# The first feed-forward in seven block products per pair of tiles, its modulation sums moved later, and one tap by ScalarE and GpSimd

## The chip, the cores and the metric

One Trainium2 chip, of which the kernel uses one core. The metric is the time of one launch in device microseconds (us). PE is TensorE, DVE VectorE, ACT ScalarE, POOL GpSimd, SP the engine that issues the DMAs.

## What is computed

Two transformer-like blocks run one after the other on 1024 positions of 1024 channels, in float32. The first ends in a feed-forward with a causal convolution of three taps over positions; the second ends in a gated feed-forward without one. D_FF is 2816.

```python
def conv_ffn(h, w_up, dw_w, dw_b, w_down):        # first block, called "f" in the kernel
    u = causal_dwconv(h @ w_up, dw_w) + dw_b      # y_t = sum_k w_k x_{t-2+k}
    gt, v = jnp.split(u, 2, axis=-1)
    return (jax.nn.silu(gt) * v) @ w_down
def swiglu(h, w_gate, w_up, w_down):              # second block, called "g"
    return (jax.nn.silu(h @ w_gate) * (h @ w_up)) @ w_down
mod = silu(c) @ mod_w + mod_b                     # 6 x 1024 columns: shifts, scales, gates
ada = silu(c_2) @ w_ada + b_ada                   # the same for the second block (and for its context)
```

## The kernel before

**Products.** Channels lie on the 128 partitions, positions along a row, so a tile is 128x1024. Each float32 operand is split into an upper part (hi, rounded to the type that TensorE takes, by ACT) and a lower part (lo, the rest, by DVE); a product is hi*hi + lo*hi + hi*lo. A tile of output channels (`tile`, `product`) takes 8 input tiles x 3 terms x 2 halves of 512 positions = 48 matmuls 128x512, the line of which is L904. Weights come by DMA into a ring of RAW = 4 places (`feed`, `raw`), ACT casts them (`wh`, L1549), DVE makes the lower part (`wl`, L2128); three tiles of these are held. PSUM has three accumulators (`ACC`, 1024 columns each) and one more area, `aux`.

**The second feed-forward (g)** has 22 pairs of tiles, gate tile n=0 and value tile n=1. The first two pairs are plain products; three of these four tiles are made "abreast" inside the normalisation that comes before (`block_end`, L950), the fourth, (1,1), by a `tile` of its own. The other 20 pairs (`PAIRS`) are taken as 2x2 block matrices in Winograd's form: seven products ("units" a11, s2, s1, s3, a12, a22, s4) of 4 input tiles x 3 terms = 12 matmuls 128x512 each (L1157), in place of eight. It needs sums of the weights (`weight_sums`, POOL, 4 per pair, 128x512, L3140), of the operand (`operand_sums`, POOL, once, L3149 to L3153) with their upper (`operand_uppers`, ACT, L1649) and lower parts (`operand_lowers`, DVE, L2448), and sums of the results (`combined`, DVE, 7 per pair, L2485). `unit_upper` (L1656) and `unit_lower` (L2453) make hi and lo of a unit's weights, up to six units ahead. Each gated result u is stored to memory by a DMA (`keep`), and read back in the down product (`load_u`, `u_upper`, `u_lower`), which comes in chunks after all pairs (`pairs_down`).

**The first feed-forward (f)** is 44 plain tiles (`ffn`). For each tile ACT multiplies by the newest tap and adds the bias (L1722), and DVE adds the two older taps from PSUM (L2551, L2554); then silu (L1726), product (L2561), hi (L1739) and lo (L2575). u stays on chip in five places, so tiles of the up and of the down product alternate (`ffn_steps`): a down chunk of 4 tiles takes 8 tiles of 24 matmuls. Between the up tiles lie the modulation sums: weight parts of 128x1024 are loaded through the same ring, and DVE adds them up (`modulation_part`, L2152 and L2155: two 128x512 instructions a part, four for the ada parts jb < 4, which carry two rows). Then PE sums over partitions (`modulation_columns`, L1123).

Every engine runs its own list in order. Where an engine waits, everything behind waits.

Of the kernel before, what the change touches and what calls it, by code (L numbers as in the profile page):

```python
# [69 lines left out]
def summed_modulations():  # L70

    parts = [("m", jb, kp) for jb in (10, 11) for kp in range(4)] + [("a", jb, kp) for jb in range(12) for kp in range(4)]
    out, at = {}, (2, 0)
    while parts:
        n = 1 if parts[0][0] == "a" and parts[0][1] < 4 else 2
        out[at], parts = parts[:n], parts[n:]
        at = (at[0], 1) if at[1] == 0 else (at[0] + 1, 0)
    return out
# [5 lines left out]
def summed_at(i):  # L84

    return [(kind, jb) for n in range(2) for kind, jb, kp in SUMMED.get((i, n), ()) if kp == 3]
# [6 lines left out]
def u_at(i):  # L93
# [14 lines left out]
    "pair_dve": ("pu2", "pu3", "pc22", "pu4", "pc11", "pc21", "pc12", "tlo2"),  # L108
    "pair_act": ("hf", "thi2", "p1c"),
    "pair_pool": ("psum", "tsum"),  # L110
# [150 lines left out]

def pool_steps(s):

    return 2 if s < 24 else 0
# [30 lines left out]
def ffn_steps():  # L295

    done = 0
    for c, fs in enumerate(CHUNKS):
        upto = min(fs[-1] + 2, FF)
        while done < upto:  # L300
            yield ("up", done)
            done += 1
        for i in range(ND if c < LAST else 0):
            yield ("dn", c, i)


# [19 lines left out]
PAIR_ORDER = list(pair_slots())  # L326

# [31 lines left out]
class Kernel:  # L359

    def __init__(self, nc, d, mem):
# [5 lines left out]
        self.pt, self.po = Ring(1), Ring(1)  # L367
        self.plan()
# [11 lines left out]
    def half_places(self):  # L380
# [3 lines left out]
        for j, (_, _, split) in enumerate(self.weights):  # L384
# [6 lines left out]
            for unit, size in made:  # L391
# [5 lines left out]
                place += size  # L397

# [44 lines left out]
    def ACC(self, *key):  # L443
        i = self.acc.slot(*key)
        return self.m.ps[:, 1024 * i:1024 * i + 1024]
# [57 lines left out]
    def PSUMS(self, n):  # L503

        return self.F(26, 512, 512 * n)

    def UNIT(self, s, i, u):

        name = UNITS[u]
        if name[0] == "s":  # L510
            return self.PSUMS("s1 s2 s3 s4".split().index(name))
# [23 lines left out]
    def operand(self, u, kk):  # L535

        hi, lo, thi, tlo = TPLACES
# [124 lines left out]
    def norm_plan(self, s):  # L662
        self.aux_take(("spread", s), [("premul", s, ND - 1)], [("premul", s, ND - 1)])
        for i in range(ND):
            self.tmp.take(("pre", s, i), ("prelo", s, i), *([("hf", s, i)] if s == "n4" else []))
# [14 lines left out]
    def ffn_plan(self, s):  # L680
        if s == "g":
            self.pair_plan(s)
            self.last_plan(s)
            return
        for step in ffn_steps():
            if step[0] == "up":
                i = step[1]
                for n in range(2):
# [2974 lines left out]
```

## Time and profile before

| what | value |
|---|---|
| median of 3 runs | 3222.43 us (3219.8 to 3224.1) |
| the profiled execution, its own time | 3218.78 us |
| its span, first to last instruction | 3217.0 us |
| PE, DVE, ACT, POOL busy | 94%, 59%, 34%, 16% |
| f, from tile (1,1) to the end of its down chunks | 623 to about 1290 us |
| g, its 20 block pairs | 2564.5 to 2945.6 us |
| mean granted clock of PE | 0.963 |

A matmul is shown with a duration of about 0.39 us, but the next one starts before it is over; the time that it costs in a full stretch is the distance from start to start. "Idle before" counts how long an engine had nothing to do ahead of a row, and the arrow names who ended that.

### The profile page before, as it was taken

What the parts mean: (1) busy time and instruction counts of PE and PEld (TensorE: products, weight loads), DVE (VectorE), ACT (ScalarE), POOL (GpSimd) and SP (SyncE); (2) the same over time, 40 slices, a digit from 0 to 9 for tenths busy, and PEclk for the clock granted to TensorE, in tenths of its full rate; (3) what the DMA queues carried; (4) which work ended last, traced back from release to release, by engine and by line L of the source; (5) the groups of instructions that cost most, each with busy time, mean ns of one, the idle gap of its engine ahead of it and who ended that gap; (6) DMA issues with size and microseconds to landing.
All of it is one profiled execution on the core that took longest, in us unless ns stands there. A gap on an engine that the chain in (4) does not pass through costs nothing. (4 is left out here: it accounts for less than half of the span.)

```text
span 3217.0 us, 33863 instructions
## 1 busy us (share of the span) xinstructions
PE 3025.4 (94%) x13510; PEld 2448.6 (76%) x13510; DVE 1911.0 (59%) x2135; ACT 1086.4 (34%) x1354; POOL 526.0 (16%) x250
## 2 busy tenths in 40 slices
PE   6999889899999999889999999899999799999997
PEld 4784467678888888768888877677777688887886
DVE  8698884755655554674521077567455866665445
ACT  3456543332222222233221133467323423233221
POOL 0598700000000000000200034000030323220000
PEclk7999889999999999999999999999998899999998
DMA  5215423231222421221332244442232222223232
GB/s 211 60 33 163 164 85 125 82 119 58 92 89 92 130 81 65 99 85 66 133 115 98 101 157 144 113 100 59 84 118 78 85 79 79 85 85 125 72 134 89
DMA packets 103556, 324.33 MB, mean 101 GB/s; under 512 B 11909, under 2 KB 15749, under 8 KB 103207
## 3 DMA queue, kind: packets, MB, share of 16 engines
q1 hardware_dynamic: 103400, 322.17, 30.2%
q8 instruction: 108, 1.77, 0.2%
q14 instruction: 48, 0.39, 0.0%
HBM read 262.87 MB, written 59.24 MB: 100 GB/s over the span
## 5 line engine op out<-in xcount | busy, mean ns | idle before, releaser
L904 PE MATMUL ps<-mainr,wh 128*128 128x512 f32 (+1 forms) x5312 | 1449.5, 390 | 28.6 <-issue 9.2
L904 PEld LDWEIGHTS ps<-mainr,wh 128*128 128x128 f32 x5312 | 995.6, 189 | 237.5 <-issue 32.0
L904 PE MATMUL ps<-mainr,wl 128*128 128x512 f32 (+1 forms) x2656 | 842.6, 389 | 0.0
L904 PEld LDWEIGHTS ps<-mainr,wl 128*128 128x128 f32 x2656 | 502.2, 189 | 103.6
L1549 ACT CAST wh<-raw 128x1024 fp32r<-128x1024 f32 (+2 forms) x272 | 238.7, 882 | 554.9 <-PE ps L904 352.4
L2128 DVE TENSOR_TENSOR wl<-raw,wh 128x1024 fp32r<-128x1024 f32 (+2 forms) x224 | 245.1, 1097 | 296.3 <-ACT wh L1549 296.0
L1157 PE MATMUL ps<-mainr,wh 128*128 128x512 f32 x1120 | 344.9, 389 | 1.5 <-DVE tmp L2468 1.5
L1157 PEld LDWEIGHTS ps<-mainr,wh 128*128 128x128 f32 x1120 | 210.2, 188 | 45.3 <-ACT wh L1656 1.9
L3109 POOL TENSOR_TENSOR tmp<-tmp,mainf 128x1024 f32<-128x1024 f32 x8 | 27.5, 3441 | 1206.1 <-DMA mainf<-in_rope 1142.2
L1157 PE MATMUL ps<-mainr,wl 128*128 128x512 f32 x560 | 217.9, 389 | 0.0
L3076 POOL TENSOR_TENSOR wl<-raw,wh 128x1024 fp32r<-128x1024 f32 x48 | 115.4, 2414 | 416.1 <-ACT wh L1549 416.1
L2620 DVE SCALAR_TENSOR_TENSOR ps<-mainf,vec,ps 128x1024 f32<-128x1024 f32 (+1 forms) x174 | 180.9, 1100 | 2.5 <-ACT ps L1842 2.3
L950 PE MATMUL ps<-mainr,wh 128*128 128x512 f32 x480 | 139.7, 415 | 34.1 <-issue 17.9
L1352 PE MATMUL ps<-mainr,wh 128*128 128x512 f32 x512 | 159.4, 393 | 6.2 <-POOL wl L3076 6.1
L950 PEld LDWEIGHTS ps<-mainr,wh 128*128 128x128 f32 x480 | 95.8, 203 | 60.0 <-issue 35.3
L2485 DVE TENSOR_TENSOR tmp<-tmp,ps 128x512 f32<-128x512 f32 x140 | 94.4, 686 | 76.0 <-PE ps L1157 74.3
L2551 DVE SCALAR_TENSOR_TENSOR tmp<-ps,vec,tmp 128x1023 f32<-128x1023 f32 x44 | 56.3, 1280 | 135.1 <-ACT tmp L1722 135.1
L2966 DVE TENSOR_REDUCE cols<-ps 128x1 f32<-128x1280 f32 x64 | 95.0, 1486 | 45.8 <-PE ps L1417 45.7
L1157 PEld LDWEIGHTS ps<-mainr,wl 128*128 128x128 f32 x560 | 105.1, 188 | 21.9
L1352 PEld LDWEIGHTS ps<-mainr,wh 128*128 128x128 f32 x512 | 96.4, 189 | 27.1 <-issue 6.8
L1722 ACT ACTIVATE tmp<-ps,vec 128x1024 f32<-128x1024 f32 x44 | 52.9, 1205 | 178.0 <-PE ps L904 178.0
L1417 PE MATMUL ps<-mainr 128*128 128x512 f32 (+1 forms) x384 | 96.2, 389 | 16.3 <-DMA mainr<-sc_k 8.4
(301 smaller groups left out, 3622.9 us busy)
## 6 DMA issues: line engine op xcount, KB each, us to landing
raw<-in_ada_w SPq DMA_DIRECT2D x48, 512.0 KB, 3.9
raw<-in_f_up SPq DMA_DIRECT2D x44, 512.0 KB, 4.4
raw<-in_g_up SPq DMA_DIRECT2D x44, 512.0 KB, 3.8
raw<-in_w_in SPq DMA_DIRECT2D x40, 512.0 KB, 4.1
raw<-in_mod_w SPq DMA_DIRECT2D x32, 512.0 KB, 4.1
raw<-in_pw SPq DMA_DIRECT2D x24, 512.0 KB, 3.8
sc_x<-mainf SPq DMA_DIRECT2D x24, 512.0 KB, 2.6
mainf<-sc_x SPq DMA_DIRECT2D x24, 512.0 KB, 7.2
```

Of the source, the lines that this page charges most:

```text
L904: ins = e.matmul(out, wt[:, a:b], xs[n], start=kk == 0 and t == 0, stop=kk == kt - 1 and t == 2)
L950: ins = e.matmul(out, wt[:, a:b], xs[n], start=kk == 0 and t == 0, stop=kk == kt - 1 and t == 2)
L1157: ins = e.matmul(k.PB(s, i, u), wt[:, 128 * kk:128 * kk + 128], xs, start=kk == 0 and n == 0, stop=kk == 3 and n == 2)
L1352: ins = e.matmul(out, wt[:, a:a + 128], x, start=first and t == 0, stop=last and t == 2)
L1417: ins = e.matmul(k.SC[i][:, a:b], k.q_at[u % 3][:, 128 * qt:128 * qt + 128], k.k_at[u % 3][t][:, a:b], start=t == 0, stop=t == 1)
L1549: e.copy(k.WH(j), k.RAWT(j)).then_inc(*k.to("whi", j))
L2128: e.tensor_tensor(k.WL(j), k.RAWT(j), k.WH(j).bitcast(F32), ALU.subtract).then_inc(*k.to("wlo_dve", j))
L2485: e.tensor_tensor(out, x, k.PB(s, i, u), ALU.add).then_inc(*k.to(name, s, i))
L2551: e.scalar_tensor_tensor(out=t[:, 1:T], in0=ps[:, 0:T - 1], scalar=k.V("fdw", 3 * f + 1), in1=t[:, 1:T], op0=ALU.mult, op1=ALU.add).then_i ...
L2620: e.scalar_tensor_tensor(out=out[:, a:b], in0=k.U(i)[:, tap + a:tap + b], scalar=k.V("dww", TAPS * i + tap), in1=k.CVP(i)[:, a:b], op0=ALU ...
L2966: e.tensor_reduce(k.STAT(n, i), k.SC[i], AX.X, ALU.max, negate=True).then_inc(*k.to("atmax", n, i))
L3076: e.tensor_tensor(k.WL(j), k.RAWT(j), k.WH(j).bitcast(F32), ALU.subtract).then_inc(*k.to("wlo_pool", j))
```

## The change

In five parts.

1. f is made as g: pairs 0 and 1 plain, pairs 2 to 21 in seven block products, u stored and read back, all down chunks behind the pairs. `ffn` and `ffn_steps` go.
2. The taps. For a pair, ACT applies the newest tap to both tiles from SBUF (`last_tap`) and multiplies the value tile by its oldest tap (`tap_product`); POOL adds that product (`second_tap`, 128x1022). DVE keeps three of four older taps (`tap`). In pairs 0 and 1 DVE does all four, from PSUM.
3. The operand sums, in f and in g, are made by DVE and not by POOL.
4. The modulation sums: m 10, 11 and ada 0 to 3 in the down steps of f; ada 4 to 11 beside the tiles `w_in` 24 to 37 of the second block.
5. Tile (1,1) of f and of g goes to `aux`, so that it doesn't wait for an accumulator; a dummy Silu after the normalisation loads ACT's table early.

```diff
 def summed_modulations():
-    parts = [("m", jb, kp) for jb in (10, 11) for kp in range(4)] + [("a", jb, kp) for jb in range(12) for kp in range(4)]
+    early = [("m", jb, kp) for jb in (10, 11) for kp in range(4)] + [("a", jb, kp) for jb in range(4) for kp in range(4)]
+    late = [("a", jb, kp) for jb in range(4, 12) for kp in range(4)]
+    steps = [(c, i) for c in range(1, LAST) for i in range(ND)]
+    for n, at in enumerate(steps):
+        out[at] = [early.pop(0)] if n < ND or n % 3 != 1 else []
+    for f in range(24, 38):
+        n = 3 if f in (26, 29, 32, 35) else 2
+        out[f], late = late[:n], late[n:]
...
+        self.beside = {("f_up", 1, 1), ("g_up", 1, 1)}
...
     def block_end(s, hi, shift, copy_free, after):
-            if n == "n4":
-                e.activation(k.F(i), k.TMP("pre", n, i), ACT.Identity, bias=shift(i)).then_inc(*k.to("hf", n, i))
+            tlo = TPLACES[{"n2": "f", "n4": "g"}[n]][3]
+            e.activation(k.F(tlo[i]), k.TMP("pre", n, i), ACT.Identity, bias=shift(i)).then_inc(*k.to("hf", n, i))
+        e.activation(k.COL("dum", 3), m.eps[RMS_EPS], ACT.Silu)
...
 # ScalarE, start of pairs_up
+        if conv:
+            operand_uppers(s, (0, 1))
+            last_tap(0, 0)
+            last_tap(0, 1)
+            operand_uppers(s, (2, 3))
+            conv_gate(0)
+            last_tap(1, 0)
+            uppers(4)
+            conv_gate(1)
+            last_tap(1, 1)
...
 # VectorE, start of pairs_up
-        operand_lowers(s, (0, 1))
-        product(0)
-        operand_lowers(s, (2, 3))
-        lowers(4)
-        product(1)
+        if conv:
+            operand_sums(s, (0, 1))
+            taps(0, 0)
+            operand_sums(s, (2, 3))
+            taps(0, 1)
+            operand_lowers(s, (4, 5, 6, 7))
+            operand_lowers(s, (0, 1, 2, 3))
+            taps(1, 0)
+            lowers(4)
+            product(0)
+            taps(1, 1)
+            product(1)
+        else:
+            operand_sums(s, range(4))
+            product(0)
+            operand_lowers(s, (4, 5, 6, 7))
+            operand_lowers(s, (0, 1, 2, 3))
+            lowers(4)
+            product(1)
...
 # GpSimd
+    def second_tap(i):
+        w.wait_ge(*k.at("cv1", i, 1))
+        w.wait_ge(*k.at("tapm", i))
+        t = k.TMP("cv", i, 1)[:, 2:T]
+        e.tensor_tensor(t, t, k.S(i % 2)[:, 0:T - 2], ALU.add).then_inc(*k.to("tapa", i))
+
+    for i in PAIRS:
+        weight_sums("f", i)
+        if i - 2 in PAIRS:
+            second_tap(i - 2)
...
-    weight_sums("g", PAIRS[0])
-    operand_sums("g", "n4")
-    for i in PAIRS[1:]:
+    for i in PAIRS:
         weight_sums("g", i)
```

The places where the order matters. First DVE's list of the kernel before at the start of f, from the last lower part of the normalisation on: the weights of tile (1,1), then the taps of pair 0 (L2551, L2554), its product and lower part.

```order
L2332 SCALAR_TENSOR_TENSOR mainr_24576_51<-tmp,cols,mainr_16384_50 128x1024
L2128 TENSOR_TENSOR wl<-raw,wh 128x1024
L2551 SCALAR_TENSOR_TENSOR tmp<-ps,vec,tmp 128x1023
L2554 SCALAR_TENSOR_TENSOR tmp<-ps,vec,tmp 128x1022
L2551 SCALAR_TENSOR_TENSOR tmp<-ps,vec,tmp 128x1023
L2554 SCALAR_TENSOR_TENSOR tmp<-ps,vec,tmp 128x1022
L2561 TENSOR_TENSOR tmp<-tmp 128x1024
L2575 TENSOR_TENSOR mainr_8192_61<-tmp,mainr_8192_61 128x1024
L2128 TENSOR_TENSOR wl<-raw,wh 128x1024
```

The same place of the changed kernel, from the operand sums of kk = 2 on (those of kk = 0 and 1 and the taps of tile (0,0) stand ahead of it): L2477 to L2481 are operand sums, L2525 taps, L2487 the lower parts of the operand sums, L2492 those of a unit's weights.

```order
L2477 TENSOR_TENSOR mainf_32768_53<-mainf_32768_53 128x1024
L2479 TENSOR_TENSOR mainf_32768_53<-mainf_32768_53 128x512
L2481 TENSOR_TENSOR mainf_32768_53<-mainf_32768_53 128x512
L2525 SCALAR_TENSOR_TENSOR tmp<-ps,vec,tmp 128x1023
L2525 SCALAR_TENSOR_TENSOR tmp<-ps,vec,tmp 128x1022
L2487 TENSOR_TENSOR mainr_32768_62<-mainf_32768_53,mainr_8192_61 128x1024 x8
L2525 SCALAR_TENSOR_TENSOR tmp<-ps,vec,tmp 128x1023
L2525 SCALAR_TENSOR_TENSOR tmp<-ps,vec,tmp 128x1022
L2492 TENSOR_TENSOR wl<-raw,wh 128x512
```

The weights of the first block product (the last row) now stand behind 12 operand sums, six taps and eight lower parts.

Then DVE's list of the changed kernel at the start of g, where the operand sums (L2477 to L2481; three more such groups are ahead of these rows) came from POOL before:

```order
L2479 TENSOR_TENSOR mainf_8192_58<-mainf_8192_58 128x512
L2481 TENSOR_TENSOR mainf_8192_58<-mainf_8192_58 128x512
L2516 TENSOR_TENSOR tmp<-ps,tmp 128x1024
L2487 TENSOR_TENSOR mainr_8192_61<-mainf_8192_58,mainr_35072_63 128x1024 x2
L2487 TENSOR_TENSOR mainr_8192_61<-mainf_8192_58,mainr_16384_50 128x1024 x2
L2487 TENSOR_TENSOR mainr_8192_61<-mainf_8192_58,mainr_32768_62 128x1024 x4
L2492 TENSOR_TENSOR wl<-raw,wh 128x512
```

Here too all eight lower parts of the operand are ahead of the first weights of a unit; twelve instructions are new on DVE and twelve are gone from POOL.

## Rows read from the trace of the kernel before

**Rows 1.** The page, part 1: busy time, share of the span, instructions.
```profile
PE 3025.4 (94%) x13510; PEld 2448.6 (76%) x13510; DVE 1911.0 (59%) x2135; ACT 1086.4 (34%) x1354; POOL 526.0 (16%) x250
```

**Rows 2.** Windows: length, busy of PE, PEld, DVE, ACT, POOL, clock, DMA.
```profile
623.00:1290.00 667.00, 660.71 (x2976) 548.55 (x2976) 370.42 (x405) 163.64 (x176) 0.00 (x0) 1.00 0.28 91
2564.50:2945.60 381.10, 381.08 (x1680) 315.31 (x1680) 232.89 (x298) 114.44 (x177) 99.46 (x73) 1.00 0.25 82
1700.00:1810.00 110.00, 110.00 (x487) 91.06 (x487) 12.25 (x10) 19.65 (x20) 0.00 (x0) 1.00 0.28 96
```

**Rows 3.** All of PE's waits from 625 to 1285 us: total, times, longest.
```profile
PE ps L904 <- ACT wh L1549: 2.5, 1, 2.5
```

**Rows 4.** PE in order of time, the start of f.
```profile
581.99 2.04 PE L950 MATMUL ps<-mainr,wh 128*128 128x512 f32 x4 [4.71 <-issue]
584.69 1.35 PE L950 MATMUL ps<-mainr,wh 128*128 128x512 f32 x4
...
620.46 0.61 PE L950 MATMUL ps<-mainr,wl 128*128 128x512 f32 x2
623.41 1.15 PE L904 MATMUL ps<-mainr,wh 128*128 128x512 f32 x4 [2.34 <-DVE tmp L2554]
```

**Rows 5.** PE in order of time, the start of g.
```profile
2496.77 2.04 PE L950 MATMUL ps<-mainr,wh 128*128 128x512 f32 x4 [4.71 <-issue]
...
2545.33 0.61 PE L950 MATMUL ps<-mainr,wl 128*128 128x512 f32 x2
2549.40 2.04 PE L904 MATMUL ps<-mainr,wh 128*128 128x512 f32 x4 [3.45 <-ACT tmp L1670]
...
2554.66 1.12 PE L904 MATMUL ps<-mainr,wh 128*128 128x512 f32 x4
...
2564.51 0.70 PE L1157 MATMUL ps<-mainr,wh 128*128 128x512 f32 x2 [1.48 <-DVE tmp L2468]
```

**Rows 6.** DVE and ACT in order of time, start of f and of g.
```profile
619.53 1.23 DVE L2128 TENSOR_TENSOR wl<-raw,wh 128x1024 fp32r<-128x1024 f32 x1 [2.94 <-ACT wh L1549]
...
2524.55 3.39 DVE L2318 TENSOR_TENSOR mainf<-mainf,mainf 128x1024 f32<-128x1024 f32 x1
...
2543.04 3.88 ACT L1649 CAST mainr<-mainf 128x1024 fp32r<-128x1024 f32 x4
2551.26 4.61 DVE L2448 TENSOR_TENSOR mainr<-mainf,mainr 128x1024 fp32r<-128x1024 f32 x4
```

**Rows 7.** POOL in order of time, operand sums at the start of g.
```profile
2516.37 2.39 POOL L3149 TENSOR_TENSOR mainf<-mainf 128x1024 f32<-128x1024 f32 x1 [31.54 <-ACT mainf L1641]
...
2523.46 3.39 POOL L3149 TENSOR_TENSOR mainf<-mainf 128x1024 f32<-128x1024 f32 x1 [1.12 <-ACT mainf L1641]
```

**Rows 8.** DVE's groups by shape, 2565 to 2945 us: busy, mean ns, idle before.
```profile
L2453 DVE TENSOR_TENSOR wl<-mainf,wh 128x512 fp32r<-128x512 f32 x77 | 63.0, 819 | 70.3 <-ACT wh L1656 69.9
L2453 DVE TENSOR_TENSOR wl<-raw,wh 128x512 fp32r<-128x512 f32 x58 | 55.0, 948 | 0.4
```

**Rows 9.** DVE's groups by shape, 640 to 1290 us.
```profile
L2155 DVE SCALAR_TENSOR_TENSOR st<-raw,cols,st 128x512 f32<-128x512 f32 x123 | 91.2, 750 | 4.8 <-DMA raw<-in_mod_w 0.5
L2551 DVE SCALAR_TENSOR_TENSOR tmp<-ps,vec,tmp 128x1023 f32<-128x1023 f32 x40 | 51.2, 1280 | 135.1 <-ACT tmp L1722 135.1
L2585 DVE TENSOR_TENSOR mainf<-mainf,ps 128x1024 f32<-128x1024 f32 x32 | 39.0, 1220 | 75.2 <-PE ps L904 75.2
L2128 DVE TENSOR_TENSOR wl<-raw,wh 128x512 fp32r<-128x512 f32 x32 | 21.9, 685 | 1.9 <-ACT wh L1549 1.9
```

**Rows 10.** ACT's group of the newest tap, 600 to 1290 us.
```profile
L1722 ACT ACTIVATE tmp<-ps,vec 128x1024 f32<-128x1024 f32 x44 | 52.9, 1205 | 178.0 <-PE ps L904 178.0
```

**Rows 11.** PE's waits at the change to g's down product, 2940 to 3110 us.
```profile
PE ps L904 <- DVE wl L2128: 1.4, 1, 1.4
PE ps L904 <- DVE mainr L2459: 1.1, 1, 1.1
```

**Rows 12.** DMA issues: KB each, median us to landing.
```profile
raw<-in_ada_w SPq DMA_DIRECT2D x48, 512.0 KB, 3.9
```

More of the change, by code:

```diff
@@ L840, in plan @@
             tmp.take(("gs", f), (f"gate{f % 2}", f))
+            self.sums_plan(f)
+            for what in summed_at(f - 1):
+                self.aux[0].take(("dmc", *what), ("mod", *what, 0))
         for o in range(2):
@@ new lines, in conv_gate, with uppers @@
+        def conv_gate(i):
+            t = k.TMP("cv", i, 0)
+            w.wait_ge(*k.at("cv", i, 0))
+            e.activation(t, t, ACT.Silu).then_inc(*k.to("us", s, i))
+        def uppers(n):
+            nonlocal made
+            for unit in PAIR_ORDER[made:n]:
+                unit_upper(s, *unit)
+            made = max(made, min(n, len(PAIR_ORDER)))
+        if conv:
+            operand_uppers(s, (0, 1))
[7 more added lines that the diff above has]
+            last_tap(1, 1)
+        else:
+            gate(0)
+            operand_uppers(s, range(4))
+            gate(1)
+            uppers(4)
@@ L1692, in pairs_up @@
+            uppers(n + 6)
+            if after:
+                if conv and u < 2:
+                    last_tap(after, 1 - u)
+                    if u == 0:
+                        tap_product(after)
+                elif conv and u == 4:
+                    conv_gate(after)
+                elif not conv and u == 1:
+                    pair_gate(after)
             if i == PAIRS[-1]:
@@ L2511, in pairs_up @@
             if u == 6:
+                if i == PAIRS[-1]:
+                    for f in CHUNKS[0]:
+                        u_lower(s, f, slots)
                 combined("pc21", i, c21, c21, 5, "pu3")
             lowers(n + 6)
+            if after and conv:
+                if u == 0:
+                    tap(after, 1, 1)
+                elif u < 3:
+                    tap(after, 0, u)
+                elif u == 5:
+                    product(after)
             if i == PAIRS[-1]:
@@ L2886, in vector_program @@
     for f in range(24, 40):
-        split_to(k.W["w_in", f] + 3)
+        split_to(k.ahead("w_in", f))
+        for what in summed_at(f - 1):
+            modulation_sum_add(*what)
     v2 = lambda ap: ap.rearrange("p (n c) -> p n c", c=512)
@@ L3390, in sync_program @@
     for f in range(24, 40):
-        feed(k.W["w_in", f] + RAW)
+        feed(max(k.W["w_in", f] + RAW, k.ahead("w_in", f)))
         if f == 24:
```

498 lines of the change are left out of this document (223 added, 275 removed).

## The prediction

> **What bounds the kernel now.** I read the page first: PE is busy 94% of the span, nobody else over 59% [rows 1]. Then the windows by stage. In f, from 623 to 1290 us, PE is busy 660.7 of 667 us at a granted clock of 1.00, DVE 370 us and ACT 164 us [rows 2]; and of PE's waits between 625 and 1285 us there is one, 2.5 us long [rows 3]. So in this stage the end is set by the number of matmuls and by nothing else. The second feed-forward shows what the new form does where it stands already: its 20 pairs take 381.1 us with 1680 matmuls and PE busy all of it [rows 2]. That is 19.06 us a pair and 0.2268 us from one matmul's start to the next. DVE is busy 232.9 us there, 11.6 us a pair, and POOL 99.5 us, 5.0 us a pair [rows 2]. Last I looked at the joints, where PE does wait: at the start of f tile (1,1) starts 2.3 us late [rows 4], and at the start of g PE idles several times up to 2564.51 us [rows 5].
>
> **The change part by part.** The sum is made against the profiled execution, 3218.8 us by its own time; the median of the runs is 3.6 us higher.
>
> *Fewer matmuls.* Twenty pairs at 84 in place of 96: 240 fewer, at 0.2268 us, **-54.4 us**. PE has no wait to hide them behind, so all of it is on the path as long as the other engines keep up.
>
> *Do they keep up inside a pair?* DVE does what it does in g (11.6 us a pair [rows 2]) and three taps at 1.28 us [rows 9], together 15.5 us. POOL's new add of 128x1022 is near its add of 128x1024, 2.39 us [rows 7], and there is a price for running it beside DVE. The row shows it: at 2524.55 DVE's add of two SBUF tiles took 3.39 us instead of 1.2, and it ended 1.1 us after POOL's instruction, which ran from 2523.46 to 2526.85 [rows 6, 7]. In g's pairs it shows in the unit lower parts: 135 of them took 118.0 us, at 0.685 us alone [rows 9] they would take 92.5, so 25.5 us, a quarter of POOL's 99.5, is DVE waiting [rows 2, 8]. At the same share the new add costs DVE 0.6 us a pair, at most its whole 2.4: 16.1 to 17.9 us, under 19.06. I take 16.5. PE runs up to five units ahead of need (13.6 us), so a late tap by itself stops nothing. ACT gets three instructions of about 1.2 us [rows 10] on top of 5.7 us a pair [rows 2]: 9.3 us. The cost to PE is nothing; the cover is 2.5 us of DVE a pair, 1.2 at the bound.
>
> The Trainium skill, SBUF — State Buffer, section "Who interferes with whom", says that a DVE instruction with two SBUF inputs contends with a GpSimd instruction that reads SBUF, each shutting the other out for its whole length. This speaks against the change, since the taps of a pair now read SBUF where they read PSUM; by the rule with every microsecond of POOL waited for, the sum would be that of the fourth rival below. The trace agrees that the lock exists.
>
> *The start of f.* Here the new order costs. Times are in the trace of before. The three tiles abreast end at 621.1 [rows 4]; tile (1,1) now starts at once, not at 623.4 (**-2.3 us**), and ends 48 matmuls later, at 632.0. The first unit needs its lower part, and DVE comes to it only after its list in the order shown. Its weights for (1,1) are done at 620.8 [rows 6]. Operand sums: one 128x1024 and two 128x512 per kk on DVE; no row has them there, the nearest are its adds, 1.2 us [rows 9] and 0.69 us, so 2.6 us. Two of them end at 626.0. The taps of (0,0) wait for ACT, which first casts the second pair of sums (2 x 0.97 [rows 6]) and then makes the newest tap (1.2 [rows 10]): 629.1. Two taps 631.7, two more sums 636.9, two taps 639.5, eight lower parts at 1.15 (four took 4.61 [rows 6]) 648.7, two taps 651.3, the first unit's lower part 652.0. PE stands still from 632.0 to 652.0, **+20.0 us**; bounds 16 (no wait for ACT) and 26 (each dependent instruction 0.2 us more). After that PE starts at the low clock. After 4.7 us idle six matmuls took 2.70 us instead of 1.36 [rows 4], after 3.4 us idle twelve took 5.3 instead of 2.7 [rows 5]: 1.3 to 2.5 us, I take **+2.0**.
>
> *From the pairs to the down product of f.* g has two waits there, 1.4 and 1.1 us [rows 11]. In f DVE and ACT have besides the last pair's taps in their lists ahead of the weights of the fourth down tile: ACT about 7.7 us after the last unit to its silu, DVE 9.0 to the product, then the copy of a result and the cast, the lower part at 10.7. PE has three down tiles of 12 matmuls ready, 8.2 us. **+2.5 us**, bounds 0 and 9.
>
> *The modulation sums.* The same instructions, moved; the columns on PE are as many. In f's down steps one ada part is four instructions of 0.75 us [rows 9], 3.0 us. A step with everything (weights 0.69, add 1.22 [rows 9], lower part of u 1.22, part 3.0) is 6.1 us against PE's 24 matmuls, 5.44; but over eight steps DVE needs 5.5 + 9.8 + 4.9 + 16 = 36.2 of 43.5 us, and weights are made two tiles ahead, so nothing waits. The ring of four places now holds two down steps: a load (3.9 us [rows 12]), the part and the weights must fit in two steps, 7.6 of 10.9 us. At `w_in` DVE is busy 12 of 110 us [rows 2]; two or three parts a tile of 10.9 us add 3 to 4.5 us. Zero for both.
>
> *The start of g.* POOL's operand sums collided with DVE's normalisation. Without them the chain runs as in f, where the tiles abreast took from 582.0 to 621.1; so in g from 2496.8 [rows 5] to 2535.9, not 2545.9. Tile (1,1) no longer waits for ACT's silu (3.45 us [rows 5]) and ends at 2546.8. Then PE waits for DVE: weights of (1,1) 2535.6, four operand sums 2546.0, product 2547.2, eight lower parts 2556.4, unit 2557.1. With 2.0 us for the clock PE has done the same work by 2559.1 instead of 2564.5: **-5.4 us**, bounds -8 and 0.
>
> *The sum.* -54.4 - 2.3 + 20.0 + 2.0 + 2.5 - 5.4 = **-37.6 us**, or 3181.2 for a profiled execution and 3184.8 for the median. I say 3185.
>
> **The rivals.**
> 1. *The joints cost more.* DVE's one list in front of f's first unit and behind its last one takes the bounds above, 26, 2.5 and 9 us, and g gains nothing: -54.4 - 2.3 + 26 + 2.5 + 9 = -19 us, 3203. For it: at these places every engine waits for another one. Chance 0.13.
> 2. *The down steps of f stall.* The cover of the sums is used up if a load takes longer than 7.2 us with three streams (weights, parts, u) at once; at 1 us a step with a part, 24 of them cost 24 us: -14 us, 3209. Against it: 3.9 us at the median [rows 12]. Chance 0.09.
> 3. *The joints are cheap.* If the sums and taps ahead of the first unit take less than the rows say, or what PE loses there is given back by waits that go elsewhere, f's start costs 8 us less and the end nothing: -48 us, 3174 (down to -60, 3162, with no gap at all). Chance 0.10.
> 4. *DVE and POOL together become the bound (slower than before).* One mechanism: the lock. POOL would work 5.0 + 2.4 = 7.4 us a pair; if DVE waited for all of it and not for a quarter, a pair took 15.5 - 1.3 + 7.4 = 21.6 us, 2.6 more than PE's, 51 us over 20 pairs: -37.6 + 51 = +13 us, 3236. It begins to count at 19.06 us a pair and ends the gain at 20.9. Against it: g's share of a quarter, and the 7 sums of results that read PSUM. Chance 0.04.
>
> The forecast has 0.64. Its own range is 3176 to 3196: the gap of f between 16 and 26, the joint between 0 and 9, g between -8 and 0, not all at one end. To hold 8 in 10 the range reaches over part of rivals 1 and 3: 3168 to 3206. 0.2% or 6.4 us is about what can be told from no change in this kernel; faster 0.92 (the forecast, 1, 3, nearly all of 2), same 0.03, slower 0.05 (rival 4 and what I don't see).
>
> **What would show it.** 1872 instead of 2112 matmuls in f's up product and pairs 19.1 us apart with PE busy throughout; DVE below 18 us a pair. One idle stretch of PE near 20 us before the first unit, ended by DVE's lower part, after a tile (1,1) without a wait. In g, no DVE add above 1.3 us in the normalisation and a gap near 10 us before the first unit. No waits of PE over 1 us in the down steps and at `w_in` 24 to 37. The prediction is wrong if pairs are further apart than 19.1 us, if PE waits for `wl` in the down steps, or if the gap is far from 20 us.

## The result

The changed kernel took 3179.95 us (median of 4 runs, 3174.6 to 3184.8), the kernel before, on the same chip, 3221.38 us (4 runs, 3219.8 to 3224.1): a ratio of 0.987 with a 95% interval of 0.9852 to 0.9889, 41 us less. The forecast was 3185 in a range of 3168 to 3206. The profiled execution took 3174.6 us, its span is 3172.8 us, 44.2 less than before.

### The profile page after: what moved, and what is told of

It reads as the page before. It is cut to its first block and busy times, and to the rows that moved or that the text cites. A ratio compares the mean times of both kernels' runs of the same rounds, so it can differ in the third digit from the quotient of the medians.

```text
span 3172.8 us, 34294 instructions
## 1 busy us (share of the span) xinstructions
PE 2968.9 (94%) x13270; PEld 2403.7 (76%) x13270; DVE 2109.6 (66%) x2387; ACT 1177.8 (37%) x1512; POOL 687.1 (22%) x338
## 5 line engine op out<-in xcount | busy, mean ns | idle before, releaser
L914 PE MATMUL ps<-mainr,wh 128*128 128x512 f32 (+1 forms) x4032 | 1104.8, 390 | 18.0 <-DVE wl L2148 8.3
L914 PEld LDWEIGHTS ps<-mainr,wh 128*128 128x128 f32 x4032 | 753.9, 189 | 175.4 <-issue 21.2
L1154 PE MATMUL ps<-mainr,wh 128*128 128x512 f32 x2240 | 693.9, 391 | 29.7 <-DVE wl L2492 19.7
L914 PE MATMUL ps<-mainr,wl 128*128 128x512 f32 (+1 forms) x2016 | 645.1, 388 | 0.0
L1154 PEld LDWEIGHTS ps<-mainr,wh 128*128 128x128 f32 x2240 | 422.7, 189 | 118.5 <-issue 30.5
L1154 PE MATMUL ps<-mainr,wl 128*128 128x512 f32 x1120 | 437.4, 391 | 0.0
L3159 POOL TENSOR_TENSOR mainf<-raw 128x512 f32<-128x512 f32 x80 | 121.7, 1521 | 659.6 <-DVE wl L2492 302.1
L1154 PEld LDWEIGHTS ps<-mainr,wl 128*128 128x128 f32 x1120 | 211.5, 189 | 44.2
L2541 DVE TENSOR_TENSOR tmp<-tmp,ps 128x512 f32<-128x512 f32 x280 | 187.7, 683 | 81.4 <-PE ps L1154 78.9
L2492 DVE TENSOR_TENSOR wl<-mainf,wh 128x512 fp32r<-128x512 f32 x160 | 135.8, 851 | 84.6 <-ACT wh L1657 84.1
L1657 ACT CAST wh<-mainf 128x512 fp32r<-128x512 f32 x160 | 99.2, 622 | 221.7 <-PE ps L1154 221.7
L2619 DVE TENSOR_TENSOR mainf<-mainf,ps 128x1024 f32<-128x1024 f32 x64 | 78.1, 1220 | 131.3 <-PE ps L914 131.2
L1355 PE MATMUL ps<-mainr,wh 128*128 128x512 f32 x512 | 159.4, 393 | 6.3 <-POOL wl L3117 6.1
L960 PE MATMUL ps<-mainr,wh 128*128 128x512 f32 x480 | 138.0, 411 | 28.8 <-issue 18.2
L1657 ACT CAST wh<-raw 128x512 fp32r<-128x512 f32 x120 | 74.6, 623 | 183.9 <-PE ps L1154 183.9
L960 PEld LDWEIGHTS ps<-mainr,wh 128*128 128x128 f32 x480 | 94.2, 199 | 54.1 <-issue 29.8
```

Source lines behind the costliest of these rows:

```text
L914: ins = e.matmul(out, wt[:, a:b], xs[n], start=kk == 0 and t == 0, stop=kk == kt - 1 and t == 2)
L960: ins = e.matmul(out, wt[:, a:b], xs[n], start=kk == 0 and t == 0, stop=kk == kt - 1 and t == 2)
L1154: ins = e.matmul(k.PB(s, i, u), wt[:, 128 * kk:128 * kk + 128], xs, start=kk == 0 and n == 0, stop=kk == 3 and n == 2)
L1355: ins = e.matmul(out, wt[:, a:a + 128], x, start=first and t == 0, stop=last and t == 2)
L1657: e.copy(k.WH(unit), k.UNIT(s, i, u)).then_inc(*k.to("whi", unit))
L2492: e.tensor_tensor(k.WL(unit), k.UNIT(s, i, u), k.WH(unit).bitcast(F32), ALU.subtract).then_inc(*k.to("wlo_dve", unit))
```

## The profile after

The page, part 1, of the changed kernel (before: [rows 1]):

```profile
PE 2968.9 (94%) x13270; PEld 2403.7 (76%) x13270; DVE 2109.6 (66%) x2387; ACT 1177.8 (37%) x1512; POOL 687.1 (22%) x338
```

PE has 240 matmuls less, all others have more to do. The windows (length, busy time of PE, PEld, DVE, ACT, POOL, clock, DMA) of f's pairs, g's pairs and the stretch with `w_in`, against [rows 2]:

```profile
654.50:1036.00 381.50, 381.49 (x1670) 315.58 (x1671) 349.60 (x360) 177.52 (x238) 176.23 (x95) 0.99 0.24 84
2519.40:2902.80 383.40, 383.34 (x1680) 316.98 (x1680) 235.59 (x301) 114.47 (x177) 104.48 (x76) 0.99 0.25 83
1634.00:1810.00 176.00, 176.00 (x814) 146.67 (x813) 64.87 (x87) 35.80 (x36) 4.79 (x2) 1.00 0.53 191
```

PE is busy all the time in each. In f DVE is busy 349.60 us in 20 pairs, 17.5 a pair, and POOL 8.8 a pair (forecast 16.5 and 7.4). PE in order of time at the two starts (f, then g; before [rows 4] and [rows 5]) and its waits over the whole span:

```profile
654.51 1.19 PE L1154 MATMUL ps<-mainr,wh 128*128 128x512 f32 x2 [19.65 <-DVE wl L2492]
2519.43 1.19 PE L1154 MATMUL ps<-mainr,wh 128*128 128x512 f32 x2 [10.04 <-issue]
```
```profile
PE ps L914 <- DVE wl L2148: 8.3, 6, 2.0
PE ps L960 <- DVE mainr L2357: 6.1, 10, 0.6
```

The first unit of f comes after 19.65 us in which PE stands still, that of g after 10.04. PE's waits for DVE in the normalisation ahead of g (L2357) are 0.6 us each; in the kernel before two of them were longer, this one and one of 2.81 us:

```profile
2524.77 2.05 PE L950 MATMUL ps<-mainr,wh 128*128 128x512 f32 x4 [3.78 <-DVE mainr L2332]
```

DVE in order of time ahead of f's first unit, in the changed kernel:

```profile
622.37 1.23 DVE L2148 TENSOR_TENSOR wl<-raw,wh 128x1024 fp32r<-128x1024 f32 x1 [2.95 <-ACT wh L1548]
...
631.94 2.60 DVE L2525 SCALAR_TENSOR_TENSOR tmp<-ps,vec,tmp 128x1023 f32<-128x1023 f32 x2 [3.17 <-ACT tmp L1687]
...
642.14 9.16 DVE L2487 TENSOR_TENSOR mainr<-mainf,mainr 128x1024 fp32r<-128x1024 f32 x8
651.22 2.60 DVE L2525 SCALAR_TENSOR_TENSOR tmp<-ps,vec,tmp 128x1023 f32<-128x1023 f32 x2
653.73 0.68 DVE L2492 TENSOR_TENSOR wl<-raw,wh 128x512 fp32r<-128x512 f32 x1
```

This is the list as it was costed: the weights of tile (1,1), the wait for ACT's newest tap, eight lower parts, two taps, the unit's lower part; from the end of the first row's instruction (623.6) to the last row's 30.8 us pass, and 31.2 were forecast (620.8 to 652.0).

**Where the time went.** Between events that both kernels have, the 44.2 us of the span are:

```
from the start to the columns in f's normalisation (565.24 -> 567.70)      +2.5
from there to the first waited matmul of L1204   (823.3 -> 776.0)         -47.3   forecast -32.2
from there to the columns in g's normalisation  (1091.4 -> 1098.7)         +7.3   forecast  0
from there to the end                            (737.1 -> 730.4)          -6.7   forecast -5.4
```

The +2.5 lies ahead of everything that the change touches; in the profiled executions of the changed kernel and its variants these columns begin at 565.5 to 570.7 us. The sum was off by 6.6 us, but the stage by stage reading was off by 15 and 7 us with opposite signs. Each row comes from one execution of each kernel. In the repetition of the changed kernel (after_again) the last three stretches are 779.9, 1096.5 and 730.6 us. So f's stretch is uncertain by some 4 us, and the one behind it took between 1096.1 and 1102.0 us over all executions of the changed kernel and of the variants that leave it alone. Within this the old and new profiles show the reasons.

First, the eight late groups of columns. In each the kernel has four float32 matmuls of 128x1, which sum a part of the modulation over the partitions; the trace shows each of them as two instructions, so eight a group and 64 in all. They stood in f and stand at `w_in` now:

```profile
1667.72 0.94 PE L1134 MATMUL ps<-ones,mainf 128*128 128x1 f32 x8
1668.53 1.19 PE L914 MATMUL ps<-mainr,wh 128*128 128x512 f32 x4
```

A group holds PE for 0.81 us (0.85 by the experiment below). Eight of them are -6.8 us in f and +6.8 us later: no gain or loss in sum, but two errors in the stage sums. (That 6.8 is so near the measured 7.3 is in part chance, by the spread above.) The forecast moved only the DVE part of this work.

Second, f's old end. The last up tile ended at 1286.7, ACT's and DVE's taps of it followed, and PE's first matmul of the last chunk came 4.09 us later, at 1290.76. PE in the kernel before, at the wait of [rows 3] and at this one:

```profile
664.28 2.05 PE L904 MATMUL ps<-mainr,wh 128*128 128x512 f32 x4 [2.54 <-ACT wh L1549]
...
1290.76 0.70 PE L904 MATMUL ps<-mainr,wh 128*128 128x512 f32 x2 [4.09 <-issue]
```

The window in which I read PE's waits ended at 1285 us [rows 3]. The two views of the prediction already disagreed: up to 1290 us PE is idle for 667.0 - 660.7 = 6.3 us [rows 2], and the one wait is 2.5. With the new order the pairs are all done before the chunks, so this wait is gone, and so are the 2.5 us of [rows 3] and 0.3 us: -6.9. The low clock behind the two waits went with them (granted clock 0.61 from 664.2 to 668 us, 0.72 from 1290 to 1296): matmuls started 0.43 us apart in place of 0.23, which cost 1.4 us behind the first wait and 1.3 behind the second.

## The experiments

In the tables "first unit" and "end" are counted from the start of the columns of 128x2 in g's normalisation (L1028, L1038 in the changed kernel) in the profiled execution.

**The changed kernel once more** (after_again).

> The changed kernel once more, to have its runs beside the variants and to see how far its runs lie apart (before they lay between 3219.8 and 3224.1, after between 3174.6 and 3184.8). My theory: the spread is in the granted clock of stretches after PE's idle times, of which this kernel has one more of 20 us; so I expect 3180 again, runs 8 to 10 us apart, and a gap of 19 to 20 us ahead of f's first unit in every trace. The rival, that the first four runs were odd: runs within 4 us.

3179.69 us (3175.1 to 3180.2), ratio 0.987 (0.9857 to 0.9884). The runs lie 5.1 us apart, between the theory's 8 to 10 and the rival's 4. The gap is 19.67 us again, so it belongs to the kernel. The first unit comes at 657.8 in place of 654.5, and the difference lies ahead of the gap: what I expected of the clock behind the gap was wrong. The span is 4.7 us longer, and 4 us of it show on PE behind f's down product. PE in order of time, first the changed kernel, then the repetition:

```profile
1294.30 1.16 PE L1081 MATMUL ps<-ident,cols 128*128 128x128 f32 x8 [0.78 <-DVE mainf L2400]
...
1312.37 1.75 PE L1051 MATMUL ps<-cols,tmp 128*128 128x2 f32 x8 [2.94 <-ACT tmp L1786]
```
```profile
1298.73 2.08 PE L1081 MATMUL ps<-ident,cols 128*128 128x128 f32 x8 [0.78 <-DVE mainf L2400]
...
1319.09 1.05 PE L1051 MATMUL ps<-cols,tmp 128*128 128x2 f32 x8 [2.93 <-ACT tmp L1786]
```

The same eight matmuls, behind the same wait of 0.78 us, take 1.16 us in one execution and 2.08 in the other, the lower level of the clock; with the work after them 18.07 us pass to the next long wait in the one and 20.36 in the other. The wait is not what lowers the clock. In both executions it falls ahead of the wait, while PE is busy and has not waited for some 240 us: the granted clock is 1.00 from 1286 to 1288 us, 0.50 from 1290 to 1292 and 0.99 from 1292 to 1294 in the changed kernel, and in the repetition 1.00 from 1288 to 1290 and 0.50 from 1290 to 1302. In the kernel before it stays at 1.00 through this work (1329 to 1341 us). The changed kernel loses 1.5 us by it ahead of the wait.

**The oldest tap back on DVE** (taps_vector).

```diff
 # GpSimd
     for i in PAIRS:
         weight_sums("f", i)
-        if i - 2 in PAIRS:
-            second_tap(i - 2)
-    for i in PAIRS[-2:]:
-        second_tap(i)
 # ScalarE
-                    if u == 0:
-                        tap_product(after)
 # VectorE
+                elif u == 3:
+                    tap(after, 1, 2)
```

> The changed kernel with the oldest tap of the value tile made by VectorE again; ScalarE's product and GpSimd's add are gone, nothing else is changed. Theory A (the matmuls bound a pair, and VectorE has just room): VectorE loses 2.4 to 2.9 us a pair of waiting for GpSimd's add and gains a tap of 1.28 us, so it is busy 16 to 17.5 us a pair, PE waits for nothing and the time is that of the changed kernel within 2 us. Theory B (the move of the tap is what makes seven products possible, VectorE being full without it): VectorE goes past 19.06 us a pair, PE waits for lower parts in the pairs, at 0.5 us a pair or more 10 us slower.

3177.26 us (3174.9 to 3178.9), ratio 0.9865 (0.9852 to 0.9879): not different from the changed kernel. The window of f's pairs in this kernel, below it DVE's group of the unit's lower parts from loaded weights (busy, mean ns), and then the same group and POOL's new one in the changed kernel:

```profile
655.60:1037.10 381.50, 381.46 (x1672) 315.74 (x1673) 350.35 (x380) 160.28 (x219) 121.23 (x76) 0.99 0.24 84
```
```profile
L2489 DVE TENSOR_TENSOR wl<-raw,wh 128x512 fp32r<-128x512 f32 x59 | 49.9, 847 | 0.0
```
```profile
L2492 DVE TENSOR_TENSOR wl<-raw,wh 128x512 fp32r<-128x512 f32 x59 | 71.6, 1214 | 0.0
...
L3165 POOL TENSOR_TENSOR tmp<-tmp,st 128x1022 f32<-128x1022 f32 x19 | 55.6, 2927 | 13.4 <-DVE tmp L2525 13.4
```

DVE is busy 350.35 us with the tap and 349.60 without it. The 19 taps that it gave away were 24.2 us (1.27 each); beside the 55.0 us that POOL works more (176.2 against 121.2) DVE waits 23.4 us more, 22 of them in these lower parts. The part of the change that its title names last, one tap by ScalarE and GpSimd, moved nothing that can be told from the spread of the runs.

**POOL's add twice** (pool_twice).

```diff
         e.tensor_tensor(t, t, k.S(i % 2)[:, 0:T - 2], ALU.add).then_inc(*k.to("tapa", i))
+        if i < FF - 2:
+            w.wait_ge(*k.at("tapa", i))
+            x = k.S(i % 2)[:, 0:T - 2]
+            e.tensor_tensor(x, x, x, ALU.add).then_inc(*k.to("tapd", i))
```

> The changed kernel with a second add of 128x1022 on GpSimd behind the tap's add in pairs 2 to 19 (it spoils the content of a scratch tile, so the next product of the tap starts from it only after it is done; the result is not changed, since the product overwrites it). GpSimd works 2.4 us a pair more. Theory A (VectorE waits for about a third of what GpSimd works): VectorE 17.5 us a pair becomes 18.3, under 19.06, no wait of PE, the changed kernel's time within 2 us. Theory B (the lock is paid in full, and VectorE is 1.5 us from being the bound): VectorE 19.9 us a pair, 18 pairs at 0.8 us, 15 us slower, with PE waiting for lower parts of units.

3183.66 us (3180.0 to 3183.7), ratio 0.9883 (0.987 to 0.9897), some 4 us more than the changed kernel in the same comparison. The window of f's pairs, and DVE's second tap:

```profile
655.40:1036.90 381.50, 378.00 (x1650) 310.52 (x1651) 370.38 (x350) 169.00 (x234) 216.20 (x113) 0.99 0.23 81
```
```profile
L2525 DVE SCALAR_TENSOR_TENSOR tmp<-tmp,vec 128x1022 f32<-128x1022 f32 x18 | 52.3, 2905 | 0.0
```

POOL works 40 us more, DVE is busy 20.8 us more: its second tap, which took 1271 ns, takes 2905. DVE is now at 370 of 381.5 us, and PE begins to wait, 3.5 us in eight waits, one a pair from 889 us on. What ends each of them is ACT's cast of a unit's weights (L1657), which stands in ACT's list behind a silu (L1704) that waits up to 8.0 us for DVE's tap: DVE's delay reaches PE through ACT. So DVE pays 43% (23.4 of 55.0 us) in the one experiment and 52% in the other of what POOL works beside it, between the quarter that the forecast took from g and the whole of the fourth rival; and 17.5 us a pair leave 1.5 us of cover. The Trainium skill, SBUF — State Buffer, section "Who interferes with whom", calls the pair of ports that the two engines share an exclusive lock, and a DVE instruction with two SBUF inputs contends for it with a GpSimd instruction that reads SBUF. The lower parts (0.85 to 1.21 us) and taps (1.27 to 2.91 us) that grow beside POOL's add agree with that; how large a share of POOL's time this costs, the page does not give; the runs do.

**The first units earlier** (units_first). The weights of the first unit are made before all operand sums are cast and lowered, and the taps of (0,1) and (1,0) behind it. In g likewise, with the first product behind the lower parts. ACT's list is reordered to match; the excerpt shows DVE's list in f alone.

```diff
 # VectorE, f
-            operand_sums(s, (0, 1))
+            operand_sums(s, (0,))
             taps(0, 0)
-            operand_sums(s, (2, 3))
-            taps(0, 1)
+            operand_sums(s, (1, 2))
+            lowers(1)
+            operand_sums(s, (3,))
             operand_lowers(s, (4, 5, 6, 7))
+            lowers(2)
+            taps(0, 1)
             operand_lowers(s, (0, 1, 2, 3))
-            taps(1, 0)
             lowers(4)
+            taps(1, 0)
```

> The changed kernel with another order of the same instructions at the start of f and g: the weights of the first two units are split between the operand sums and their lower parts, ScalarE makes the newest taps of pair 0 first, the taps of tile (1,0) come behind the lower parts. Theory A (what PE waits for is only the length of VectorE's list ahead of the first unit): in f the first unit starts right behind tile (1,1), the second at about 642 and the third at about 650 us in the time of the first trace, so PE is 9 to 10 us ahead; in g the first unit fits in the gap, and the second starts at about 2551, 4 to 5 us ahead. In all 13 to 15 us faster than the changed kernel, less 2 for the clock: 3167. Theory B (the gap has another cause, the stores or ScalarE): the gap stays near 20 us and the time near 3180.

3163.73 us (5 runs, 3160.5 to 3168.4), ratio 0.9825 (0.9812 to 0.9839), 16 us less than the changed kernel. PE in f, later in the same kernel:

```profile
643.35 0.91 PE L1154 MATMUL ps<-mainr,wh 128*128 128x512 f32 x2 [4.70 <-DVE wl L2494]
651.00 1.19 PE L1154 MATMUL ps<-mainr,wh 128*128 128x512 f32 x2 [3.07 <-issue]
```

The gap of 19.65 us has become waits of 4.70 and 3.07 us, that of g two of 2.3 and 2.5. So the gap was made by the order of the lists (DVE's, with ACT's along with it), not by the amount of work.

**Both: first units early, taps on DVE** (best: the two edits together).

> The order of units_first (3163.7 us, 16 faster than the changed kernel) together with the oldest tap on VectorE as in taps_vector (2.4 us faster than the changed kernel, which is within the spread of the runs). If the two are independent and the second is real: 3161. If the second is noise: 3164. If ScalarE and GpSimd were needed for the tap when PE has less idle time to catch up in (VectorE enters the pairs with its list less far ahead): PE waits in the first pairs, 3166 or more.

3159.3 us (3159.0 to 3161.4), ratio 0.9815 (0.98 to 0.983): the fastest version by its median, 60 us or 1.9% under the kernel before in the same set of runs (3219.31 us), and without the tap on ScalarE and GpSimd. The intervals of this ratio and of units_first (0.9812 to 0.9839) overlap, so that giving the tap back gains anything is not shown.

**The late columns once** (late_columns_once). This kernel leaves out three quarters of eight sums of the modulation over the partitions, so its output is not the reference's: one matmul of 128x4 stands for four of 128x1 in each of the eight late groups (two instructions in the trace for eight).

```diff
+        if kind == "a" and jb >= 4:
+            src = k.MSUM(kind, jb, 0)[:, 0:128]
+            e.matmul(ps[:, 3072:3076], src, m.ones[:, 0:4], start=True, stop=True).then_inc(*k.to("dmc", kind, jb))
+            return
```

> The changed kernel with one matmul in place of four in each of the eight sums over partitions that moved to the tiles w_in 24 to 37 (it leaves out three quarters of those sums, so the shifts, scales and gates that come from ada 4 to 11 are not the reference's). In the trace f became 47 us shorter and the part behind it, up to the normalisation of g, 7.3 us longer. Theory A (the 7.3 us are the eight groups of columns themselves, 0.9 us each, which f no longer has): 8 x 0.6 = 5 us faster than the changed kernel, and that part 2 us longer than before the change. Theory B (the loads and VectorE's parts beside w_in slow something down): no change.

3171.33 us (3169.5 to 3172.0), ratio 0.985, span 3169.3. PE at the first group and at the last, and below it the last one of the changed kernel:

```profile
1667.89 0.28 PE L1134 MATMUL ps<-ones,mainf 128*128 128x4 f32 x2
...
1800.17 0.28 PE L1134 MATMUL ps<-ones,mainf 128*128 128x4 f32 x2
```
```profile
1804.96 0.94 PE L1134 MATMUL ps<-ones,mainf 128*128 128x1 f32 x8
```

Between the first and the last group 132.28 us pass in place of 137.24: 0.71 us for each of seven groups. The one with four columns itself takes 0.14 us (1800.17 to the next start, 1800.31), so a group of four single columns costs 0.85. The medians differ by 8 us, the spans by 3.5, and eight groups give 5.7; I don't read more into the medians, as the medians of the kernel before differ by 3.4 us from set to set of runs (3218.3 to 3221.7).

**Tile (1,1) without a place of its own** (no_beside).

```diff
-        self.beside = {("f_up", 1, 1), ("g_up", 1, 1)}
+        self.beside = set()
```

> The changed kernel with tile (1,1) of f and of g in the accumulator of tile (0,0) again, the other units' halves moved along. My sum priced this at 2.3 us in f. Looked at again, the first unit waits for VectorE's list at 652 whenever tile (1,1) ends before that, so in f a later tile (1,1), which must now wait for both taps of (0,0), 634.5, only eats into the gap: first unit at the same time, 0 us. The rival, the price as I had it: 2 us slower; or more, if the units' halves are now free later.

3178.67 us (3175.3 to 3180.4), ratio 0.9872. PE at f's start:

```profile
635.57 2.04 PE L914 MATMUL ps<-mainr,wh 128*128 128x512 f32 x4 [10.77 <-DVE tmp L2522]
655.40 1.19 PE L1151 MATMUL ps<-mainr,wh 128*128 128x512 f32 x2 [7.04 <-issue]
```

One gap of 19.65 us has become two of 10.77 and 7.04, and the first unit starts 87.2 us behind the columns of f's normalisation in place of 86.8. The 2.3 us that the forecast booked for the missing wait of tile (1,1) buy nothing by themselves: whatever PE does early ahead of this gap, the gap grows by.

**g's operand sums back on POOL** (g_sums_pool).

```diff
 # VectorE, g
-            operand_sums(s, range(4))
             product(0)
 # GpSimd
+    weight_sums("g", PAIRS[0])
+    operand_sums("g", range(4))
```

> The changed kernel with g's operand sums made by GpSimd again, behind its weight sums of pair 2, as in the kernel before; f keeps them on VectorE. My theory (the 5.4 us of g came from this move alone): adds of the normalisation in g take up to 3.4 us again, tiles abreast end 10 us later; tile (1,1) now waits for nothing, VectorE's list ahead of the first unit is 10.4 us shorter; so the first unit starts about 5 us later than in the changed kernel, counted from the first tile abreast, with a gap of some 5 us ahead of it, minus what the shorter gap spares at the low clock: 3 to 5 us slower. The rival, that the early load of ScalarE's table and the place of tile (1,1) in aux made the gain: same time as the changed kernel within 1 us.

3176.35 us (3175.5 to 3178.3), ratio 0.9867: not slower, against what I expected. DVE's groups of the normalisation in this kernel, the first of them in the changed one, and then PE in order of time in this kernel:

```profile
L2343 DVE TENSOR_TENSOR mainf<-mainf,mainf 128x1024 f32<-128x1024 f32 x8 | 16.3, 2038 | 0.0
...
L2350 DVE SCALAR_TENSOR_TENSOR tmp<-mainf,cols,ps 128x1024 f32<-128x1024 f32 x8 | 10.2, 1281 | 0.3
```
```profile
L2343 DVE TENSOR_TENSOR mainf<-mainf,mainf 128x1024 f32<-128x1024 f32 x8 | 9.8, 1220 | 0.0
```
```profile
2492.98 2.05 PE L960 MATMUL ps<-mainr,wh 128*128 128x512 f32 x4 [3.78 <-DVE mainr L2357]
...
2525.41 0.70 PE L1154 MATMUL ps<-mainr,wh 128*128 128x512 f32 x2 [0.34 <-issue]
```

The waits in the normalisation are back as they were before (DVE's adds of two SBUF tiles take 2038 ns in place of 1220; L2350, which reads PSUM, is as short as ever), but the gap of 10.04 us ahead of the first unit is gone, and PE is at the high clock there. The first unit comes 77.2 us behind the columns in place of 77.0, and the end 728.2 us in place of 730.4. The 2.2 us lie behind the first unit, where PE runs at the low clock after the gap. Moving these sums to DVE has therefore cost 2.2 us in the changed kernel (with the same start of g the stretch to the end took 730.1 to 730.6 us in five executions: the changed kernel, its repetition, taps_vector, pool_twice and late_columns_once); the gain at g's start must be from something else.

**g's start, further back.** With the sums on POOL and no place for (1,1) (g_pool_no_beside: the last two edits together):

> In g both parts of the change at its start are undone: POOL makes the operand sums again and tile (1,1) has no place of its own (in f the sums stay with DVE, tile (1,1) has no place of its own either). From the columns in g's normalisation to the end of the kernel it was 737.1 us before and 730.4 after; with the sums alone back on POOL 728.2, with the place alone gone 730.0. Theory A, each of the two alone brings the gain and the two overlap, because each takes away the same wait of PE for ACT and DVE behind the tiles abreast: with both gone the stretch is 736 to 738 us again and the time near 3186 us, 7 us more than with the change. Theory B, the stretch is shorter for another reason, such as the order of DVE's list behind the normalisation: it stays at 728 to 731 us and the time at 3177 to 3180 us.

3175.14 us (3171.3 to 3182.2), ratio 0.987 (0.9851 to 0.9888): the stretch to the end is 727.9 us, theory B. So neither is it. What still differed was the order of the lists of ACT and DVE, with the load of the silu's table:

```diff
-        e.activation(k.COL("dum", 3), m.eps[RMS_EPS], ACT.Silu)
+        if n != "n4":
+            e.activation(k.COL("dum", 3), m.eps[RMS_EPS], ACT.Silu)
 # ScalarE, g
+            operand_uppers(s, (0, 1))
             gate(0)
-            operand_uppers(s, range(4))
+            operand_uppers(s, (2, 3))
             gate(1)
 # VectorE, g
+            operand_lowers(s, (4, 0, 5, 1))
             product(0)
-            operand_lowers(s, (4, 5, 6, 7))
-            operand_lowers(s, (0, 1, 2, 3))
+            operand_lowers(s, (6, 2, 7, 3))
```

> Everything at the start of g as before the change: operand sums on POOL, no place of its own for tile (1,1), and besides the lists' order: ACT casts four of the operand's sums before the first silu and loads the silu's table only there, DVE makes four lower parts before the first product. With the sums on POOL and no place of its own but the new order of the lists, 727.9 us passed from the columns in g's normalisation to the end; before the change 737.1. Theory A, the order of ACT's and DVE's lists is what shortened g's start: 736 to 738 us here, PE waits 3.5 us for ACT's silu, and the time is near 3185 us. Theory B, what shortened it is something else that all versions of the changed kernel have: 728 us and 3175 to 3178 us.

> The changed kernel with only ACT's list at g's start as before: the first silu behind four casts of the operand's sums, the silu's table loaded there; sums on DVE, tile (1,1) with its own place. Theory A, with tile (1,1) in its own place no matmul waits for that silu, but DVE's first product does, behind its sums, and DVE's list up to the first unit sets PE's gap of 10.0 us: the casts of the first two sums fit in the 10.4 us in which DVE makes its sums, so the stretch to the end stays at 730.4 us or gets up to 1 us longer, time 3178 to 3181 us. Theory B, the order of ACT's list sets the gap here too: 734 to 737 us and 3184 to 3187 us.

The first (all of it) took 3178.12 us (3177.7 to 3178.9), the second (only ACT's part, the rest as changed) 3180.86 us (3174.0 to 3186.2). In the first PE and ACT at g's start:

```profile
2512.94 2.04 PE L914 MATMUL ps<-mainr,wh 128*128 128x512 f32 x4 [4.67 <-ACT tmp L1669]
```
```profile
2506.58 3.88 ACT L1648 CAST mainr<-mainf 128x1024 fp32r<-128x1024 f32 x4
2510.48 1.28 ACT L1669 ACT_TABLE_LOAD   x1
2511.77 1.02 ACT L1669 ACTIVATE tmp<-ps 128x1024 f32<-128x1024 f32 x1
```

The wait of [rows 5] for ACT's silu is back, 4.67 us, behind four casts and a table load. Each kernel with the time from the columns to the first unit and to the end of the span:

```
kernel             first unit    end
before                84.6      737.1
g_old_start           81.7      732.4
g_pool_no_beside      77.3      727.9
g_sums_pool           77.2      728.2
no_beside             76.8      730.0
after                 77.0      730.4
g_old_act             77.2      730.5
```

The new order of ACT's and DVE's lists, with the early table load, is worth 4.5 us where tile (1,1) waits for the silu (732.4 against 727.9); these three were undone together, so what each gives is not shown. ACT's part alone is worth nothing where tile (1,1) doesn't wait (730.5 against 730.4). 4.7 us between g_old_start and the kernel before remain. 2.9 lie ahead of the first unit: the low clock behind the wait for the silu lasted for six matmuls more before, 1.2 us, and there was a wait of 1.48 us for DVE's product [rows 5] that isn't there any more (units and tiles have other places in PSUM now, which would explain it; no run undid them). 1.8 lie behind it, 1.4 of them at the change to g's down product, where two waits of 1.08 and 1.43 us [rows 11] have become one of 1.56; why is not shown.

**The fastest version with g's sums on POOL** (best_pool: the edits of best and of g_sums_pool).

> The version with the first units early and the taps on DVE, and g's operand sums by POOL. Theory A, what counts is DVE's whole list up to g's first unit and POOL takes 10.4 us from it while DVE waits some 9 us for POOL in the normalisation: a gain of about 2 us as with the sums alone on POOL, so 3157 us. Theory B, the wait of PE in the tiles abreast (11 us in all, where the sums ran on POOL) is only hidden while a gap of 10 us stands behind it; here that gap is 5 us, so 3 to 5 us are lost: 3163 us.

3163.66 us (3156.4 to 3166.1), ratio 0.9827 (0.9813 to 0.9842). From the columns to the end 727.4 us pass, in the fastest version 726.0. This agrees with theory B in sign: POOL's sums gained 2.2 us where PE has a gap of 10 us behind the waits in the normalisation, and lose 1.4 where the waits behind them are 4.7 us. The size is less than theory B said, it rests on one execution of each, and the rest of the 4 us between the medians is within what medians of one kernel differ (the intervals of the two ratios overlap).

## Why the prediction was right

The mechanism was right: PE's matmuls bound f, and the one long gap is made by DVE's list. That the start of g came out within 1.3 us of its term is luck, since the cause was another one.

*Fewer matmuls, -54.4 us.* Right: 240 instructions less on the page, and the 20 pairs last 383.9 us from the first unit to the wait behind them (654.51 to 1038.44), which is 1680 times 0.2268 us, 381.0, and 2.9 of the clock.

*DVE keeps up.* Right in the outcome, mis-sized: 17.5 us a pair in place of 16.5, inside the bounds of 16.1 and 17.9. The term that was off is the lock's share: a quarter of POOL's time, taken from g, where taps_vector and pool_twice measured 43% and 52%. So the add costs DVE 1.2 us a pair (23.4 over 19 adds), where 0.6 were booked. Besides, the first tap of each tile (128x1023) takes 1.62 us in place of 1.28, in taps_vector too: 0.7 us a pair. And POOL's add is 2.93 us in place of 2.39. Fourth rival: fallen, at 92% of PE's time for a pair. It would begin earlier than at the 100% that it names: in pool_twice PE waited with DVE at 97%.

*The start of f, +20.0 and +2.0 us.* 19.65 us, and 2.9 us for the clock together with the work behind it. The list added up instruction by instruction is the best term of the sum. The -2.3 us of tile (1,1) is right as booked (the gap is counted from that tile's end) and no gain of its own, as no_beside shows.

*Pairs to the down product, +2.5 us.* 1.09 and 1.85 us, 2.9 in sum.

*The modulation sums, 0.* Right in total. In the stages wrong by 6.8 us each way, since PE's columns move with them.

*Not in the sum at all:* 6.9 us of waits in the old f, because the window that I asked for ended at 1285 us, two microseconds ahead of the largest of them. f's parts are then -54.4 -2.3 +19.7 +2.9 +2.9 -6.8 -6.9 = -44.9 of the measured -47.3. The low clock behind the two old waits adds -2.7 and the low clock at the end of the new down product +1.5, together -46.1; the last 1.2 us are not assigned.

*The start of g, -5.4 us.* Measured -6.7, and the reason was wrong. The step that failed is "POOL's operand sums collided with DVE's normalisation. Without them the chain runs as in f": the chain does run 10 us earlier, but DVE's list then makes a gap of 10.04 us, and the move by itself costs 2.2 us (measured in the changed kernel; no run makes this move alone in the kernel before). What gained was the order of the lists around the first silu with the early table load, 4.5 us: the prediction let the wait for the silu go, but gave the whole term to the sums. 4.7 us more have no cause that an experiment shows: 4.5 and 4.7 less 2.2 for the sums and 0.3 for the place of tile (1,1) are the 6.7.

Of the rivals the third, "the joints are cheap", is nearest in time, since the old waits of f went, not because the joints got cheaper. The median stands 5 us under the forecast, within its own range.

## What to carry to other kernels

Ask for the waits of a stage up to the next one's first instruction and a little beyond: a wait at the seam belongs to neither window if each ends early. And compare the sum of the waits with the idle time of the same window: here 2.5 stood against 6.3 us. Give work to POOL only if DVE's remaining list reads PSUM or the cover is large: here 55 us on POOL took 24 us of work off DVE and gave it 23 us of waiting. When a chain's start is costed, add up the list in order as it stands, and then try the list in another order: the first consumer's inputs ahead of the rest gave 16 us, more than a third of the whole change.

## What the runs showed of the hardware

Two executions of one kernel differ in the clock that PE is granted at the same place: behind the same wait of 0.78 us, at the end of f's down product, eight matmuls of 128x128 took 1.16 us in eight of the 14 profiled executions and some 2.08 in six (after_again, best, best_pool, no_beside, g_sums_pool, g_old_act), 2 to 4 us of the span. The clock had fallen 5 to 7 us ahead of that wait in 12 of the 14, with PE busy and without a wait for some 240 us; in the kernel before and in pool_twice it didn't fall there. It is of the size of the effects at g's start, and the reason that these were read between events and not from medians.

Four float32 matmuls with a single column each (eight instructions in the trace), between large ones, cost 0.85 us, and one with four columns 0.14 (two instructions). A DVE instruction with two SBUF inputs took up to 3.4 us in place of 1.2 beside one of POOL, and the tap took 2.9 in place of 1.27 in the mean; the one that reads PSUM (L2350) stayed at 1.28, also where an instruction of POOL that reads SBUF ran beside it (2488.09 us in g_sums_pool).
